# An eight-way output projection replaced by seven products per pair of row tiles, and the state-space stage placed between other gate groups

## The chip, the cores and the metric

The kernel runs on one core of a Trainium2 chip. The metric is the device time of one execution in microseconds (us), from the first to the last instruction of the core. TensorE is PE in the rows, VectorE is DVE, ScalarE is ACT, GpSimd is POOL, and SyncE is SP. SP issues most of the transfers, in one queue in the order in which they are written.

## What is computed

It is one step of a one-layer hybrid decoder for 512 prompt rows and 64 sample rows (576 rows of 1024 values, all in float32). What matters here, with `h = rms_norm(x)`:

```python
z = h @ w_in
u, q, kvc, kvs, kvw, g_nsa, g_a, g_b = jnp.split(z, cuts, axis=-1)
y_ssm, ssm_state = s5_scan(u, h0, ...)          # states, 64 wide, in 32 groups of 16 channels
zg = jax.nn.gelu(y_ssm)
glu = zg * jax.nn.sigmoid(zg @ w_glu + b_glu)
o_nsa = nsa_attention(qh, gh, full_c, full_s, win_ext, ...)
a_br = glu @ w_ssm_out
b_br = o_nsa @ w_nsa_out
merged = jax.nn.sigmoid(g_a) * a_br + jax.nn.sigmoid(g_b) * b_br
x = x + merged @ w_o                              # 576 x 1024 by 1024 x 1024
x = x + hier_moe(rms_norm(x), ...)                # 16 experts, top 2 in one of 4 groups
x = x + jax.nn.sigmoid(x @ w_ple_gate) * (p_l @ w_ple)
y = rms_norm(x) * final_norm_g
```

`s5_scan` has no matrix form of its own. The kernel cuts the 576 rows into 72 chunks of 8 and turns the inside of a chunk into small products, and walks over the chunks with a recurrence on VectorE.

## The kernel before

**One queue per engine.** Every engine runs its own list in the order in which it is written, and the engines meet at semaphores. The TensorE list is the spine. Its results go to a ring of six PSUM banks (`begin` takes the next bank once it has been emptied, `finish` counts up `pe_done`), and `make_plan` says for each result which engine empties it. A row tile is 128 rows (tiles 0 to 3) or 64 rows (tile 4, the samples). Weights pass through three buffers, `w_slot0` to `w_slot2`, in the order of the table `WEIGHTS`. A load waits until the last product with the buffer's former contents is done.

**The input projection and the state-space stage.** After the u and the key and value columns TensorE works through eight gate groups m = 0 to 7 (`gate_products(m)`: ga and gb for 128 features each, two halves of 288 rows, 32 matrix products) and four query groups (`query_products(m, h)`). The short products of the state-space stage stand between them: `x` (transposes of the u rows, which SP has read back from DRAM in chunks as `uc` and VectorE has copied into `ucg`), `vt` (transposes of the input maps `vn`), `k` (the taps, from `bbar` and `gm`), `d` (the drive of each chunk). Then VectorE walks over the 64 prompt chunks, a loop of five short instructions a step, while TensorE does the other gate and query groups, and `y` (the outputs) waits for the walk (`walked`). `KD_A` is the number of gate groups ahead of `x`. `gm`, the output maps, is made by seven GpSimd instructions of 2304 values, at the same time as VectorE makes `bbar` and `vn`. After `y` twelve transposes of no use (`keep_busy(12)`) stand before `zg` (transposes of the activated outputs), then come `fin` and `glu`.

**What follows the last gate group.** The normalized input `hT` is read by the gate groups. Its space is used again for the raw cache pages of the attention stage, so SP holds them back:

```python
            sp.wait_ge(pe_done, PLAN.done(("gb", KD - 1, 1)))
            for s in range(NSEQ):
                load_raw(s)
```

Behind the 16 page loads (`load_raw`, lines 795 and 799, with a table entry read into a register for each) SP issues `pe_r`, `w2`, the weights `w1k0` and `w1k1` (line 723), and at last the final states as two outputs, which count up `fin_out` (lines 814 and 816). ScalarE, VectorE and GpSimd wait for `fin_out` before they write to buffers of the attention stage (in ScalarE's list `act.wait_ge(fin_out, 32)` stands ahead of the first copy into `kvct`). TensorE's transposes `pe` (line 1334) and `ct` 0 to 9 (line 1342) fill at most six banks before ScalarE empties the first, and the compression products (line 1365) need the last `ct` copied.

**The output projection and the router.** `merged` is made on VectorE in 16 pieces from the products `ab` and `bb`. Then `through_w_o(t, c)` makes 128 rows by 512 columns with eight products of 512 columns each, for tiles 0 to 3 and the two halves c of `w_o` (buffers `wo0`, `wo1`), and one group for tile 4 (`("wo", 4, 1)`). `add_w_o` adds each to `x` on VectorE with the factor 0.25. The four halves c = 0 come first. `second_norm_steps` is the table that mixes the rest with the second norm and the router: `xT` (transposes of x), `rt` and `rb` (router logits), `pT` and `pp` (the per-layer embedding), `rank`, `first`, `list` (the sorting of rows by expert). `NORM2` is the order in which the tiles are normalized: ScalarE squares a tile, GpSimd makes the root, ScalarE scales (`hn`), GpSimd writes the rows to DRAM (`h_rows`). When the last tile is written and the first expert's row list is made, GpSimd gathers the first expert's rows, SP waits for them (`hg_ld[0]`) and only then loads the third and later experts' weights.

## Time and profile before

| what | value |
|---|---|
| three timed runs | 814.77, 816.21, 816.44 us (median 816.21) |
| span of the profiled execution | 820.2 us (no other time is recorded for it) |
| TensorE busy | 789.7 us, 96% of the span |
| VectorE, ScalarE, GpSimd busy | 345.2, 193.6, 138.9 us |
| mean granted TensorE clock | 0.992 |
| bytes moved | 136.49 MB, 166 GB/s over the span |

Busy time of TensorE is near the whole span, so the reader looks for the places where TensorE waits and for what stands behind each wait. The profiled execution is 4.0 us longer than the median of the timed ones.

### The profile page before, as it was taken

To read this page: it belongs to the slowest core of one execution; us is meant where nothing else is said; L and a number is where in the kernel's file an instruction comes from. 1 tells how busy PE (TensorE), PEld (TensorE's weight loads), DVE (VectorE), ACT (ScalarE), POOL (GpSimd) and SP (SyncE) were. 2 spreads that over 40 slices of the span, in tenths; PEclk is the share of its full clock that TensorE was granted. 3 is DMA by queue.
4 is the path that set the end of the run, shared out by engine and by line. 5 is a ranking of instruction groups with operands and counts; after the bars stand their busy time and mean duration, and the time that the engine had idled before them with its cause. 6 is when DMAs were issued, how large, how long until landed. Compare 5 with 4: busy or idle time off the path is not lost. (4 is left out here: it accounts for less than half of the span.)

```text
span 820.2 us, 13714 instructions
## 1 busy us (share of the span) xinstructions
PE 789.7 (96%) x5151; PEld 513.4 (63%) x5151; DVE 345.2 (42%) x944; ACT 193.6 (24%) x462; POOL 138.9 (17%) x167
## 2 busy tenths in 40 slices
PE   8999999999999999898999999999999999999995
PEld 6455577877778879655666775445556564554441
DVE  2279911365553332666734363123732101115433
ACT  3010211311111344554523200035211111122222
POOL 3029300500001211234510100012111101014000
PEclk9999999999999999999999999999999999999998
DMA  9540294551411396800030179003699999996011
GB/s 323 146 123 0 81 280 164 145 46 40 172 44 43 109 175 225 225 1 2 1 117 2 59 219 370 2 26 116 226 420 414 418 417 416 416 353 206 26 51 39
DMA packets 81221, 136.49 MB, mean 166 GB/s; under 512 B 33926, under 2 KB 57546, under 8 KB 76946
## 3 DMA queue, kind: packets, MB, share of 16 engines
q1 hardware_dynamic: 64636, 110.17, 40.9%
q0 software_dynamic: 3728, 13.38, 4.6%
q10 hardware_dynamic: 12798, 12.12, 4.4%
q8 instruction: 41, 0.67, 0.3%
q14 instruction: 18, 0.15, 0.1%
HBM read 116.55 MB, written 21.19 MB: 168 GB/s over the span
## 5 line engine op out<-in xcount | busy, mean ns | idle before, releaser
L1170 PE MATMUL ps<-hT,w_slot 128*128 128x288 f32 x640 | 156.2, 407 | 0.0
L1170 PEld LDWEIGHTS ps<-hT,w_slot 128*128 128x128 f32 x640 | 121.3, 190 | 34.1 <-issue 0.8
L1170 PE MATMUL ps<-w_slot,hT 128*128 128x512 f32 (+1 forms) x320 | 127.0, 555 | 0.3 <-DVE hT L1835 0.3
L1170 PEld LDWEIGHTS ps<-w_slot,hT 128*128 128x128 f32 x320 | 60.0, 190 | 61.0 <-issue 42.4
L1170 PE MATMUL ps<-w_slot,merged 128*128 128x512 f32 x128 | 55.9, 593 | 0.0
L1674 PE MATMUL ps<-w_slot,hT 128*32 128x256 f32 x544 | 49.7, 380 | 0.0
L2624 DVE SCALAR_TENSOR_TENSOR th<-th,ps 128x256 f32<-128x256 f32 x12 | 5.1, 422 | 105.2 <-ACT th L2077 105.2
L1170 PEld LDWEIGHTS ps<-w_slot,merged 128*128 128x128 f32 x128 | 24.0, 190 | 28.4 <-issue 28.2
L1043 POOL TENSOR_TENSOR hT<-hT,w_p 128x512 f32<-128x512 f32 (+3 forms) x11 | 25.1, 2282 | 51.2 <-DVE w_p L2150 51.2
L1170 PE MATMUL ps<-qg,w_slot 128*128 128x288 f32 x128 | 33.7, 408 | 0.0
L1674 PEld LDWEIGHTS ps<-w_slot,hT 128*32 128x32 f32 x544 | 26.3, 110 | 10.0 <-issue 2.3
L2410 DVE TENSOR_REDUCE nm_p<-ps 128x2 f32<-128x256 f32 (+3 forms) x32 | 24.9, 819 | 15.9 <-PE ps L1415 15.8
L1170 PE MATMUL ps<-onsaT,w_slot 128*128 128x288 f32 x128 | 31.2, 406 | 0.0
L1662 PE MATMUL ps<-wgu,hT 128*128 128x256 f32 x128 | 28.9, 382 | 0.9 <-DVE hT L2150 0.9
L1674 PE MATMUL ps<-wgu,hT 128*32 128x256 f32 x352 | 28.4, 379 | 0.6 <-DMA w_slot<-in_w_exp_up 0.6
L1985 ACT ACTIVATE hT<-ps,nm_p 128x128 f32<-128x128 f32 (+3 forms) x44 | 22.6, 524 | 25.9 <-DVE nm_p L2410 21.8
L984 POOL TENSOR_SCALAR stat<-stat 128x1 f32<-128x1 f32 (+1 forms) x15 | 3.0, 203 | 151.3 <-ACT qg L2022 93.2
L1170 PEld LDWEIGHTS ps<-onsaT,w_slot 128*128 128x128 f32 x128 | 24.3, 190 | 6.7
L1662 PEld LDWEIGHTS ps<-wgu,hT 128*128 128x128 f32 x128 | 23.9, 190 | 6.7 <-issue 2.5
L2498 DVE SCALAR_TENSOR_TENSOR x<-ps,x 128x512 f32<-128x512 f32 x8 | 5.5, 692 | 50.0 <-PE ps L1170 50.0
L1104 POOL TENSOR_TENSOR tick<-tick 128x1 f32<-128x1 f32 x16 | 3.1, 195 | 138.6 <-PE ps L1645 90.2
L1170 PEld LDWEIGHTS ps<-qg,w_slot 128*128 128x128 f32 x128 | 23.2, 191 | 5.4
(441 smaller groups left out, 1223.1 us busy)
## 6 DMA issues: line engine op xcount, KB each, us to landing
merged<-in_w_exp_down SPq DMA_DIRECT2D x11, 1024.0 KB, 17.1
w_slot<-in_w_in SPq DMA_DIRECT2D x8, 1024.0 KB, 6.9
wgu<-in_w_exp_gate SPq DMA_DIRECT2D x8, 1024.0 KB, 12.8
wgu<-in_w_exp_up SPq DMA_DIRECT2D x8, 1024.0 KB, 15.1
w_slot<-in_w_exp_gate SPq DMA_DIRECT2D x8, 1024.0 KB, 13.1
w_slot<-in_w_exp_up SPq DMA_DIRECT2D x8, 1024.0 KB, 15.6
expert_rows<-onsaT ACTq DMA_DIRECT2D x12, 512.0 KB, 8.0
w_slot<-in_w_exp_down SPq DMA_DIRECT2D x5, 1024.0 KB, 16.1
```

The source lines that it names most:

```text
L984: link(pool.tensor_scalar(stat[0:p, 1, t:t + 1], stat[0:p, 0, t:t + 1], 1.0 / D, EPS, ALU.mult, ALU.add))
L1043: pool.tensor_tensor(p4, p4, w_p[:, i].rearrange("p a b -> p (a b)").unsqueeze(2).broadcast_to([P, 4, n]), ALU.mult).then_inc(pr_scaled, 1)
L1104: pool.tensor_tensor(tick[:, 1:2], tick[:, 0:1], tick[:, 0:1], ALU.add).then_inc(pool_tick, 1)
L1170: ins = pe.matmul(out, a, b, start=(n == 0), stop=(n == len(pairs) - 1))
L1662: ins = pe.matmul(ps[:, 2 + u, FF * w:FF * w + FF], hgT[:, u, k], w0[:, w, k], start=(k == 0), stop=(k == KD - 1))
L1674: ins = pe.matmul(ps[g:g + 32, 2 + u, FF * w:FF * w + FF], hgT[:, u, k, g:g + 32], gate_up_slot(l)[:, w, k], start=(k == 0), stop=(k == KD ...
L1985: ins = act.activation(probs[i % PBUFS][:, (2 * c + kh) * n:(2 * c + kh) * n + n], ps[:, 2 * (at % 2) + kh, 0:n], ACT.Exp, bias=nm_p[:, at ...
L2410: dve.tensor_reduce(nm_p[:, at], ps[:, 2 * (at % 2):2 * (at % 2) + 2, 0:n], axis=X, op=ALU.max, negate=True).then_inc(pr_max, 1)
L2498: empty(dve.scalar_tensor_tensor(v, o[0:TILES[t], :], 0.25, v, ALU.mult, ALU.add))
L2624: dve.scalar_tensor_tensor(th[:, u], th[:, u], 1.0, ps[:, 2 + u, 0:FF], ALU.add, ALU.mult).then_inc(si_made, 1)
```

## The change

There are two parts. **In the state-space stage** `KD_A` goes from 3 to 1: gate group 0 alone stands before `x`, group 1 comes after `d`, groups 2 to 6 after the queries, and group 7 stands behind `y`, where `keep_busy(12)` was. SP issues the read of `uc` ahead of the query weights (it was behind the key and value outputs), loads gate weights `g2` after the taps and `glu` ahead of `g3`. `gm` is made by six VectorE instructions behind `vn` in place of the seven on GpSimd, and the staging of the first gates moves from `xg` to `vt`. **In the output projection** the rows of a pair of tiles (0 and 1, 2 and 3) and the four quarters of `w_o` are combined so that seven products of four matrix products each (128 rows, 512 values of the sum, 512 columns) replace eight of them: 56 matrix products in all in place of 64. Four of a pair's products accumulate in a bank of their own (`ps[:, RING + p]`) with an addition to x between them. VectorE makes the sums (`row_sum`, and four combinations of weights of 2048 values each). Tile 4 goes first, NORM2 becomes (4, 0, 1, 2, 3), and the table mixes the products with the router in a new order. The final gain `gf` and the first two down weights are loaded after `("rt", 2)`.

```diff
-KD_A = 3
+KD_A = 1
...
+    steps = [("wo", 4, 1), ("m", 0, 1), ("m", 0, 2), ("xT", 4, 0), ("xT", 4, 1), ("m", 1, 1), ("rt", 4, 0), ("m", 1, 2), ("rb", 4, 0)]
+    steps += [("m", 0, 5), ("m", 0, 6), ("m", 0, 3), ("m", 0, 7), ("xT", 0, 0), ("xT", 0, 1), ("m", 0, 4), ("rt", 0, 0)]
+    steps += [("m", 1, 5), ("rb", 0, 0), ("xT", 1, 0), ("m", 1, 6), ("xT", 1, 1), ("pT", 0, 0), ("pT", 1, 0), ("m", 1, 3), ("rt", 1, 0)]
+    steps += [("pT", 2, 0), ("pT", 3, 0), ("m", 1, 7), ("rb", 1, 0), ("pT", 4, 0), ("xT", 2, 0), ("xT", 2, 1), ("xT", 3, 1), ("m", 1, 4)]
+    steps += [("rt", 2, 0), ("xT", 3, 0), ("rb", 2, 0), ("pp", 0, 0), ("rt", 3, 0), ("pp", 0, 1), ("rb", 3, 0), ("pp", 1, 0), ("rank", 0, 0)]
+    steps += [("pp", 1, 1), ("first", 0, 0), ("pp", 2, 0), ("list", 0, 0)]
+    return steps + [("pp",) + job for job in PP_JOBS[5:len(PP_JOBS) - PP_LEFT]]
...
+AFTER_W_O = ("rt", 2)
...
             load_weights("g0")
             load_weights("g1")
+            sp.wait_ge(u_out, 16 * NT)
+            sp.wait_ge(v_made, 1)
+            sp.wait_ge(g_made, 1)
+            sp.dma_start(uc, u_dram.rearrange("(c t) n -> c t n", t=CH)).then_inc(uc_ld, 16)
             load_weights("q")
...
-            load_weights("g2")
...
+            load_weights("g2")
+            load_weights("glu")
             load_weights("g3")
-            load_weights("glu")
...
+            gate_products(KD_A)
             for m in range(1, GQA):
                 for h in range(2):
                     query_products(m, h)
-            for m in range(KD_A, KD):
+            for m in range(KD_A + 1, KD - 1):
                 gate_products(m)
             pe.wait_ge(walked, 1)
...
-            keep_busy(12)
+            gate_products(KD - 1)
             pe.wait_ge(y_gelu, 8)
...
+            def w_o_product(p, i):
+                a, b = (slice(P * (2 * p + t), P * (2 * p + t) + P) for t in range(2))
+                low, high = wk("wo0", 512), wk("wo1", 512)
+                rows, weights = {1: (merged[:, 0:4, a], low[:, 0:4]), 2: (merged[:, 4:8, a], low[:, 4:8]), 3: (s_wo[:, 3], high[:, 4:8]),
+                                 4: (merged[:, 4:8, b], low[:, 4:8]), 5: (s_wo[:, 0], t1_wo), 6: (s_wo[:, 1], t2_wo),
+                                 7: (s_wo[:, 2], high[:, 0:4])}[i]
+                if i in (5, 6, 7, 3):
+                    pe.wait_ge(wo_sums, 4 * p + {5: 1, 6: 2, 3: 3, 7: 4}[i])
+                if i in (5, 6, 7, 4):
+                    pe.wait_ge(wo_weights, {5: 1, 6: 2, 7: 3, 4: 4}[i])
+                before = {6: 1, 7: 6, 4: 7, 3: 5}.get(i)
+                if before:
+                    pe.wait_ge(wo_added, ADDED.index((p, before)) + 1)
+                if i == 2:
+                    o = begin(("wo2", p, 2))
+                elif i == 5:
+                    o = begin(("wo2", p, 3))
+                elif i == 3:
+                    o = bank(("wo2", p, 3))
+                else:
+                    o = ps[:, RING + p]
+                for k in range(4):
+                    ins = pe.matmul(o, rows[:, k], weights[:, k], start=(k == 0 and i in (1, 2, 5)), stop=(k == 3), skip_group_check=True)
+                if i in (2, 3):
+                    finish(ins)
+                else:
+                    ins.then_inc(wo_chain, 1)
...
+            n9 = [P, NS, CH + 1, GRP]
+            pr, pi = (pw[:, :, r, :].rearrange("p t s -> p s t").unsqueeze(3).broadcast_to(n9) for r in range(2))
+            c_re, c_im = (cst[:, r].unsqueeze(2).broadcast_to(n9) for r in range(2))
+            tg9 = tmp_g.rearrange("p (s t c) -> p s t c", s=NS, t=CH + 1)
+            tt(gm[:, 0], pr, c_re, ALU.mult)
+            link(tt(tg9, pi, c_im, ALU.mult))
+            tt(gm[:, 0], gm[:, 0], tg9, ALU.subtract)
+            link(tt(gm[:, 1], pi, c_re, ALU.mult))
+            link(tt(tg9, pr, c_im, ALU.mult))
+            dve.scalar_tensor_tensor(gm[:, 1], gm[:, 1], -1.0, tg9, ALU.mult, ALU.subtract).then_inc(g_made, 1)
...
+            def row_sum(p, i):
+                a, b = (slice(P * (2 * p + t), P * (2 * p + t) + P) for t in range(2))
+                low_a, high_a, low_b, high_b = merged[:, 0:4, a], merged[:, 4:8, a], merged[:, 0:4, b], merged[:, 4:8, b]
+                n = 4 * p + {5: 1, 6: 2, 3: 3, 7: 4}[i]
+                first, second, op = {5: (low_b, high_b, ALU.add), 6: (s_wo[:, 0], low_a, ALU.subtract),
+                                     3: (high_a, s_wo[:, 1], ALU.subtract), 7: (low_a, low_b, ALU.subtract)}[i]
+                tt(s_wo[:, {5: 0, 6: 1, 7: 2, 3: 3}[i]], first, second, op).then_inc(wo_sums, 1)
+                dve.wait_ge(wo_sums, n)
+            row_sum(0, 5)
+            for n in range(2):
+                dve.wait_ge(*w_need[f"wo{n}"])
+            tt(t1_wo, high[:, 0:4], low[:, 0:4], ALU.subtract).then_inc(wo_weights, 1)
+            dve.wait_ge(wo_weights, 1)
+            row_sum(0, 6)
+            tt(t2_wo, high[:, 4:8], t1_wo, ALU.subtract).then_inc(wo_weights, 1)
+            dve.wait_ge(wo_weights, 2)
+            row_sum(0, 3)
+            row_sum(0, 7)
...
+            def add_product(p, i):
+                a, b = 2 * p, 2 * p + 1
+                places = {1: [(a, 0)], 2: [(a, 0)], 5: [(b, 1)], 6: [(a, 1)], 3: [(a, 1)], 7: [(b, 1)], 4: [(b, 0)]}[i]
+                if i in (2, 3):
+                    o = take(("wo2", p, i))
+                else:
+                    dve.wait_ge(wo_chain, CHAINED.index((p, i)) + 1)
+                    o = bank(("wo2", p, 3)) if i == 5 else ps[:, RING + p]
+                n = ADDED.index((p, i)) + 1
+                dve.wait_ge(wo_added, n - 1) if n > 1 else None
+                t, c = places[0]
+                v = x[:, t, 512 * c:512 * c + 512]
+                ins = dve.scalar_tensor_tensor(v, o, 0.25, v, ALU.mult, ALU.add).then_inc(wo_added, 1)
+                if i in (2, 3):
+                    dve.wait_ge(wo_added, n)
+                    dve.sem_inc(drained["dve"], 1)
+                return ins
...
+                    add_last_rows()
+                    tt(high[:, 0:4], high[:, 4:8], high[:, 0:4], ALU.subtract).then_inc(wo_weights, 1)
+                elif what == "m":
+                    add_product(t, c)
+                    if (t, c) == (1, 2):
+                        tt(low[:, 4:8], low[:, 4:8], t2_wo, ALU.subtract).then_inc(wo_weights, 1)
+                    elif t == 0 and c in (5, 6, 3, 7):
+                        row_sum(1, c)
```

TensorE, the end of the state-space stage, before: the last `y` products (`vn,xg` and `gm,hst`), the twelve idle transposes, and `zg`, `fin`, `glu`.

```order
L1300 MATMUL ps<-vn,xg 72x128 x8
L1306 MATMUL ps<-gm,hst 72x128 x16
L1188 MATMUL ps<-ident 128x128 x12
L1315 MATMUL ps<-ident,uc 128x72 x32
L1319 MATMUL ps<-ident,fin 128x128 x2
L1321 MATMUL ps<-ident,fin 16x128 x2
```

The same place of the changed kernel, where the row with `hT` is gate group 7:

```order
L1302 MATMUL ps<-vn,xg 72x128 x8
L1308 MATMUL ps<-gm,hst 72x128 x16
L1171 MATMUL ps<-hT,w_slot 128x288 x32
L1317 MATMUL ps<-ident,uc 128x72 x32
L1321 MATMUL ps<-ident,fin 128x128 x2
L1323 MATMUL ps<-ident,fin 16x128 x2
```

The last reader of `hT` has moved from in front of all `y` products to behind them.

SP's queue from the weights of gate group 2 and 3 on (`w_slot1`), before. The 16 rows of line 707 are the query weights.

```order
L695 DMA w_slot1<-in_w_in 128x8x256 x2
L707 DMA w_slot2<-in_w_in 128x4x64 x16
L752 DMA out_2<-kv 128x4x256
L755 DMA out_6<-kv 64x256
L752 DMA out_3<-kv 128x4x256
L755 DMA out_7<-kv 64x256
L752 DMA out_4<-kv 128x4x256
L758 DMA out_8<-kv 8x256 x8
L760 DMA out_8<-in_cache_win_kv 8x4x16384
L767 DMA uc<-u_rows 72x4096
```

And changed:

```order
L713 DMA w_slot1<-in_w_in 128x8x256 x2
L770 DMA uc<-u_rows 72x4096
L725 DMA w_slot2<-in_w_in 128x4x64 x16
L774 DMA out_2<-kv 128x4x256
L777 DMA out_6<-kv 64x256
```

The read of `uc` now stands between two sets of weights, directly ahead of the query weights.

TensorE, the output projection, before: behind the last product from `onsaT` come four halves, then `x` transposes between the others (L1177 is tile 4, L1600 and L1605 the router).

```order
L1170 MATMUL ps<-w_slot,merged 128x512 x32
L1590 MATMUL ps<-ident,x 128x128 x4
L1170 MATMUL ps<-w_slot,merged 128x512 x8
L1590 MATMUL ps<-ident,x 128x128 x4
L1170 MATMUL ps<-w_slot,merged 128x512 x8
L1590 MATMUL ps<-ident,x 128x128 x8
L1177 MATMUL ps<-w_slot,merged 64x512 x16
L1600 MATMUL ps<-hT,w_rt 32x128 x8
```

And changed, where `onsaT` holds the row sums, `qg` and `kv` the weight sums, and L1579 is `w_o_product`:

```order
L1178 MATMUL ps<-w_slot,merged 64x512 x16
L1579 MATMUL ps<-w_slot,merged 128x512 x8
L1622 MATMUL ps<-ident,x 128x64 x8
L1579 MATMUL ps<-w_slot,merged 128x512 x4
L1632 MATMUL ps<-hT,w_rt 32x64 x8
L1579 MATMUL ps<-w_slot,merged 128x512 x4
L1637 MATMUL ps<-groups_sum,actT 64x20
L1579 MATMUL ps<-qg,onsaT 128x512 x4
L1579 MATMUL ps<-kv,onsaT 128x512 x4
L1579 MATMUL ps<-w_slot,onsaT 128x512 x8
```

Tile 4, which needs all of `merged` and both halves of the weights, has become the first group, and the products follow in fours.

## Rows read from the trace of the kernel before

**Rows 1.** The page: span, busy time by engine, transfer rate in 40 slices.

```profile
span 820.2 us, 13714 instructions
...
PE 789.7 (96%) x5151; PEld 513.4 (63%) x5151; DVE 345.2 (42%) x944; ACT 193.6 (24%) x462; POOL 138.9 (17%) x167
...
GB/s 323 146 123 0 81 280 164 145 46 40 172 44 43 109 175 225 225 1 2 1 117 2 59 219 370 2 26 116 226 420 414 418 417 416 416 353 206 26 51 39
```

**Rows 2.** Chain that ended last, in time: start, length, engine or transfer.

```profile
573.56 6.57 DMA h_rows<-hn
...
580.69 4.69 DMA hT<-h_rows,idx
...
587.02 10.88 DMA w_slot<-in_w_exp_up
```

**Rows 3.** TensorE timeline, gate groups 0 to 2, transposes x, drive d.

```profile
96.30 46.83 PE L1170 MATMUL ps<-hT,w_slot 128*128 128x288 f32 x192
142.96 2.17 PE L1251 MATMUL ps<-ident,qg 72*128 72x72 f32 x32
...
158.53 4.22 PE L1285 MATMUL ps<-xg,vt 128*64 128x72 f32 x128
```

**Rows 4.** TensorE timeline from the first y products to the compression.

```profile
263.66 1.91 PE L1300 MATMUL ps<-vn,xg 128*72 128x128 f32 x16
...
278.80 1.53 PE L1188 MATMUL ps<-ident 128*128 128x128 f32 x12
...
284.07 15.76 PE L1170 MATMUL ps<-vt,w_slot 128*128 128x288 f32 x64 [0.50 <-DVE vt L2333]
...
307.42 2.46 PE L1365 MATMUL ps<-kvct,w_slot 128*128 128x161 f32 x16 [1.05 <-ACT kvct L1858]
```

**Rows 5.** SP's issues: query weights, raw pages, compression weights, later pages.

```profile
97.45 14.18 SPq L707 DMA_DIRECT2D w_slot<-in_w_in  x16
...
264.92 18.10 SPq L799 DMA_DIRECT2D hT<-in_cache_cmp_kv  x16
...
285.62 8.06 SPq L723 DMA_DIRECT2D w_slot<-in_cmp_w  x4
...
303.38 18.50 SPq L826 DMA_DIRECT2D caches<-in_cache_slc_kv  x16
```

**Rows 6.** ScalarE timeline, the first copies of the attention stage.

```profile
302.23 5.14 ACT L1858 ACTIVATE kvct<-ps 128x64 f32<-128x64 f32 x11 [1.86 <-DMA out<-fo_p]
```

**Rows 7.** VectorE timeline: small operations, last of vn, copy of uc, end of the walk.

```profile
64.44 9.42 DVE L2150 TENSOR_TENSOR sm<-sm 128x16 f32<-128x16 f32 x3
...
103.56 2.27 DVE L2150 TENSOR_TENSOR vn<-vn,uc 128x2048 f32<-128x2048 f32 x1
...
139.11 2.29 DVE L2275 COPY qg<-uc 72x4096 f32<-72x4096 f32 x1 [33.08 <-DMA uc<-u_rows]
...
257.11 0.31 DVE L2324 TENSOR_TENSOR fin<-fin,cst 128x144 f32<-128x144 f32 x1
```

**Rows 8.** GpSimd timeline, the last of the seven instructions that make gm.

```profile
83.47 6.06 POOL L1006 TENSOR_SCALAR gm<-gm 128x2304 f32<-128x2304 f32 x1
```

**Rows 9.** Line 707, the query weights: time from issue to landing.

```profile
DMA to landing us min/median/max: 3.5/4.3/8.0
```

**Rows 10.** Windows (PE, PEld, DVE, ACT, POOL busy; clock; DMA share; GB/s).

```profile
133.00:135.00 2.00, 2.00 (x10) 1.56 (x9) 0.00 (x0) 0.00 (x0) 0.00 (x0) 1.00 0.52 184
...
336.00:337.00 1.00, 0.93 (x5) 0.78 (x6) 0.01 (x1) 0.99 (x5) 0.00 (x0) 0.50 1.03 201
```

**Rows 11.** TensorE timeline of the output projection: first four, one xT.

```profile
501.25 27.63 PE L1170 MATMUL ps<-w_slot,merged 128*128 128x512 f32 x64
...
568.24 0.64 PE L1590 MATMUL ps<-ident,x 128*128 128x128 f32 x4
```

**Rows 12.** VectorE timeline, last piece of merged, addition of the last product.

```profile
502.01 0.46 DVE L2150 TENSOR_TENSOR merged<-mt 128x288 f32<-128x288 f32 x1
...
568.30 0.69 DVE L2498 SCALAR_TENSOR_TENSOR x<-ps,x 128x512 f32<-128x512 f32 x1 [6.64 <-PE ps L1170]
```

153 lines of the change are left out of this document (71 added, 82 removed).

## The prediction

> **What bounds the kernel now.** I read the page first: TensorE is busy 96% of a span of 820.2 us [rows 1]. So time is won by taking work from TensorE or its waits, and it is lost wherever TensorE is made to wait. Next I read the chain that ended last. Its last part starts at the second norm: the write of the normalized rows, the gather of the first expert's rows, the load of expert weights that SP holds back until the gather has landed [rows 2]. Behind it the expert stage moves 414 to 420 GB/s in six slices on end [rows 1], so transfers pace it as much as TensorE does. A gain ahead of that stage counts only as far as the gather comes earlier. Third I read TensorE's timeline around each edited place, and then the queues of the engines that release it. There the reader is to see one thing above all: a second chain, which TensorE does not show as a wait because its own work is just as long.
>
> That chain starts when the last gate group has been computed, since the raw cache pages go where `hT` was. In the trace TensorE goes on to y at 263.66 [rows 4]. SP starts the page loads 1.26 us later, at 264.92, and spends 18.10 us on 16 of them, 1.13 us each. That price does not depend on the place, as the later 16 pages cost 18.50. At 285.62 come the compression weights, 8.06 us [rows 5], then the final states as outputs, for whose landing ScalarE waits until 302.23 with the first copy into kvct [rows 6]. The copies take 5.14 us, and the compression starts at 307.42, after only 1.05 us of visible idle time [rows 4]. So from the end of the gates to the compression there are 307.42 − 263.66 = 43.76 us of a chain of SP and ScalarE. TensorE has filled it with y (15.14 us, up to 278.80), the idle transposes, zg, fin, 15.76 us of glu [rows 4], and the transposes.
>
> **The change part by part.**
>
> *Group 7 behind y.* All y products move in front of the gates' end. With an otherwise unchanged list that end falls at 278.80 in place of 263.66: +15.14 us. The 43.76 us behind it are all issues, landings and copies that this edit leaves as they are, so the compression starts 15.14 us later too. TensorE then has only zg, fin and glu as cover, to about 19.5 us after the gates' end (the 15.76 of glu and what stands from 278.80 + 1.53 to 284.07), the transpose pe and five banks of ct. Then it waits for ScalarE's first copy, which comes 302.23 − 263.66 = 38.57 us after the gates' end. What is late next is everything: VectorE and GpSimd wait for the same landing, and the caches' loads stand behind it in SP's queue. The idle transposes (1.53 us) that go away are worth nothing, as the glu stage no longer ends on the path. Neither does the earlier walk gain: it needs to 257.42 [rows 7], y stood at 263.66, and now it has some 25 us of slack that nobody uses.
>
> *One gate group ahead of x.* TensorE reaches x at 96.30 + 46.83/3 = 111.91, not at 142.96 [rows 3]. For that u must be back in chunks. Today uc lands at 139.1 [rows 7]. Two things move it forward. VectorE's small operations ran at about 3 us each, as in 9.42 us for three, while GpSimd made gm, to 89.53 [rows 7, 8]; without these neighbours the part up to vn is shorter by some 30 us. I take it so that vn is done near 76 instead of 105.8. The six new VectorE instructions have 2304 values; at 2.27 us for 2048 [rows 7] they take 2.55 us each, 15.3 in all, so gm is there at about 91, ahead of SP's 97.45 [rows 5]. That edit I cost at nothing. But uc (1.18 MB) now goes in front of the query weights. Those are issued from 97.45 for 14.18 us [rows 5] and the last lands at 111.6 + 3.5 or later [rows 9], 115.1; TensorE wants them after x, at 111.9 + 2.0 = 113.9. The bare lateness is 1.2 us. To it comes the time of uc: at the 420 GB/s of the best slice [rows 1] 2.8 us; at the 184 GB/s while uc itself was moving [rows 10] 6.4 us, and the landing may be the median 4.3 instead of 3.5. That gives a wait between 1.2 (uc beside the others) and 8.4 us. I take 5.5, between the two prices of uc. The copy of uc, 2.29 us [rows 7], ends close to TensorE's arrival and stays under this wait.
>
> The Trainium skill (DMA: Bandwidth & Descriptors, section Why a DMA increments its semaphore by 16 and not by 1) says that a transfer is spread over the largest number of engines up to 16 that divides its outer dimension. For the 72 rows of uc these would be 12, and an estimate by that page with three quarters of the best rate is 3.7 us for uc, a wait of 4.9 us. The 0.52 share of the engines in that window neither shows nor excludes it [rows 10].
>
> *The clock.* After short idle times the granted clock is 0.50 in the slice from 336 [rows 10], that is 1.2 in place of 2.4 GHz, and three such slices follow each other. Two long waits are new. I price the first at 1.5 us (three slices at half rate), the second at 1.0, since ScalarE paces the transposes there. Bounds: 0 and 4 together.
>
> *Seven products in place of eight.* Four whole products take 27.63 us with the overlap of one, thus 3.4 us for four matrix products [rows 11]. 56 instead of 64 matrix products save 6.9 us of TensorE. At the start, tile 4 needs the last piece of merged, which ends at 502.47 [rows 12] while TensorE is free at 501.25 [rows 11]: 1.3 us lost. Row sums of 512 values (0.7 us, like an addition of 0.69 of that size) and weight sums of 2048 (2.3 us [rows 7]) are on VectorE, which sat idle 6.64 us ahead of such an addition [rows 12]; the first such product comes some 22 us after the merge, 9 us of sums are ready by then. The chained bank needs each addition (0.7 us) before the next product into it, and other work of 3.4 us stands between, except at product 4 of the first pair, where two xT of up to 0.64 us each [rows 11] cover about all. So no further wait there.
>
> But what counts is the last tile. Before, the last product ended at 568.2, as its addition starts at 568.30 [rows 12], and the rows' write was issued at 573.56, 5.4 us later [rows 2]. In the new table five pT (two transposes each), one more xT (four, 0.64 us with its overlap [rows 11]), one rt and two rb stand ahead of the last product. I take them at 0.27 us each on average, 2.4 us: it ends at 568.2 − 6.9 + 1.3 + 2.4 = 565.0. Behind it ScalarE's list has the copies of tile 2 and 3 ahead of the squares of tile 3. The copy of tile 3 waits for its transpose, and this for rt of tile 2, which waits for ScalarE too. That costs 1.3 us more than before. The write then starts at 565.0 + 5.4 + 1.3 = 571.7 against 573.56: about 1.9 us earlier, and I take 2.0. The first expert's list is ready a little sooner than the write, as before. The gather, the weights behind it and the expert stage come 2.0 us earlier. The other 3.6 us of TensorE's saving become idle time ahead of the experts. Bounds: 0 (the saving is all eaten by the added steps) and 6.9 − 1.3 = 5.6 us.
>
> **The sum** against the profiled span: 15.1 + 5.5 + 2.5 − 2.0 = +21.1 us, 841.3. The span is 4.0 us above the median of the runs, 816.21; I take the difference as it is: 837.3 us. Ends: 15.1 + 1.2 + 0 − 5.6 = +10.7, 826.9; 15.1 + 8.4 + 4.0 − 0 = +27.5, 843.7.
>
> **Rivals.** A: all of TensorE's saving in the projection arrives, since the write's 6.57 us and the gather also shorten or the lists don't block. For it: TensorE alone is then 5.6 us earlier. Against it: ScalarE's order. 833.7 us, chance 0.12. B: the projection gives nothing, because VectorE's additional 14 us of sums delay the additions. Against it: the 6.64 us of idle time ahead of an addition [rows 12]. 839.3 us, 0.10. C: gm on VectorE comes late, because the operations are slow for another reason than GpSimd: vn at 105.8, gm at 121, uc and the query weights 23 us later than assumed. TensorE then waits until some 139, and the whole is 17 us more than forecast, 855 us. The end of the slow operations together with GpSimd's last speaks against it [rows 7, 8]. 0.06. D, the other side: SP's chain gets shorter once nothing but zg and glu runs beside it, page loads at half their cost and the 8.06 us of weight issues nearly gone. It decides from the point where page loads to fin_out take under about 22 us in place of 37; then TensorE bounds the start of the compression, group 7 only changes places with y, and the idle transposes (1.5 us) are saved. With query weights nearly in time (1.2) and 2.0 to 5.6 us of the projection that is 816.2 − 1.5 + 1.2 − 3.8 = 812.1. The unchanged 1.13 to 1.16 us a page at two places with different neighbours [rows 5] speaks against it. 0.04. That the edit does not delay the pages at all is excluded by the list: the semaphore counts results in order, and group 7 is behind y.
>
> **How the numbers follow.** The forecast has 0.68. Its own range by the bounds is 827 to 844, which holds A and B as well, so 828 to 844 leaves out C, D and the tails, under 2 in 10. A measurement of this kernel can tell about 0.2% (1.6 us) from no change. Faster by more: D, 0.04. Within: 0.01. Slower: 0.95.
>
> **What would show it.** In the changed trace: the last gate product ends near 285; SP's first page load 1.3 us behind it; TensorE idle for some 13 us at the ct transposes, released by ScalarE's kvct copy, and about 3 us at pe; the compression 43 to 45 us behind the gates' end, near 330. Before that, a wait of about 5 us at the first query product for the weights, gm on VectorE done at 91, no VectorE operation of 16 values over 0.3 us. In the projection: 3.4 us for four matrix products, 1.3 us of wait at tile 4, the write of the last tile 2 us closer to the end of bb than now (72.3 us), and idle time ahead of the first expert. The prediction is wrong if the compression follows the gates' end in much less than 43 us, or if the distance from bb's end to the first expert shrinks by more than 4 us.

## The result, and the profile of the changed kernel

The changed kernel takes 845.37 us in the median of 4 runs (843.72 to 849.00), against 816.33 us for the kernel before (4 runs beside it): ratio 1.0344, 95% interval 1.0315 to 1.0373. That is 29.0 us slower. The prediction said 837.3 us, 21.1 us slower, with a range of 828 to 844: the sign was right, the size was 8 us too small, and the time lies 1.4 us outside the range. The run that was profiled took 849.0 us, the slowest of the four, with a span of 847.3 us, 27.1 us more than the span before. First the page: span, busy time by engine, the transfer rate in 40 slices.

```profile
span 847.3 us, 13694 instructions
...
PE 790.6 (93%) x5123; PEld 512.9 (61%) x5123; DVE 347.5 (41%) x968; ACT 194.0 (23%) x462; POOL 107.2 (13%) x160
...
GB/s 332 122 119 0 143 224 106 175 80 29 141 43 15 66 128 210 229 106 1 1 33 80 2 186 356 61 14 64 236 403 410 419 416 416 417 363 183 27 50 37
```

TensorE is busy as long as before (790.6 against 789.7 us) in a span that is 27.1 us longer [rows 1]. It has less work now, so part of this busy time is a lower clock; the loss is waits and what the clock costs behind them, and the timeline of TensorE says where they are. This is the beginning, after the first gate group (start, length; in brackets the idle time ahead and what ended it).

```profile
112.55 2.23 PE L1252 MATMUL ps<-ident,qg 72*128 72x72 f32 x32 [1.83 <-DVE qg L2327]
120.46 6.43 PE L1171 MATMUL ps<-hT,w_slot 128*128 128x288 f32 x16 [5.68 <-DMA w_slot<-in_w_in]
126.73 3.66 PE L1264 MATMUL ps<-ident,vn 128*128 128x128 f32 x32
```

Two waits, 1.83 us for the copy of `uc` and 5.68 us for the query weights, and behind the second the 16 query products take 6.43 us where they take 4.15 at full clock. The window over them shows why: granted clock 0.59, so most of them ran at the lower level of 1.2 GHz after the idle time (columns as in [rows 10]; the second window is from the later, longer wait).

```profile
121.00:126.00 5.00, 5.00 (x13) 3.51 (x12) 0.00 (x0) 0.00 (x0) 0.00 (x0) 0.59 0.69 236
311.00:322.00 11.00, 2.28 (x13) 2.04 (x11) 0.00 (x0) 0.00 (x0) 0.00 (x0) 0.66 1.39 164
```

What is behind the first wait is in VectorE's row, and behind the second in SP's: `uc` is issued at 96.15 and its copy starts at 110.20, 14.05 us later; the 16 transfers of the query weights take 20.01 us to issue, where they took 14.18 [rows 5].

```profile
95.03 0.99 SPq L713 DMA_DIRECT2D w_slot<-in_w_in  x2
96.15 1.33 SPq L770 DMA_DIRECT2D uc<-u_rows  x1
97.53 20.01 SPq L725 DMA_DIRECT2D w_slot<-in_w_in  x16
...
110.20 2.29 DVE L2327 COPY qg<-uc 72x4096 f32<-72x4096 f32 x1 [11.85 <-DMA uc<-u_rows]
```

The first row is a neighbour that matters: two loads of gate weights, 2 MB together, issued just ahead of `uc` in the same queue. The trace also has the packets of the transfers. `uc` travels in 72 packets of 16,384 bytes, and the two windows below count none of them from 96 to 102 us and all of them from 102 to 109.5 (the packets of 8 KB or more are 1109 − 1037 = 72).

```profile
DMA packets 1934, 1.96 MB, mean 327 GB/s; under 512 B 16, under 2 KB 1934, under 8 KB 1934
DMA packets 1109, 1.59 MB, mean 212 GB/s; under 512 B 843, under 2 KB 1037, under 8 KB 1037
```

So of the 14.05 us some 6.0 are the wait behind the gate weights, 7.3 the packets of `uc` (102.2 to 109.5), and 0.7 the rest. The packets of the query weights (256 bytes each) last from 102.4 to 120.0 us, 17.5 us, where they took 10.7 before (103.6 to 114.2). The 6.8 us more are nearly the 7.3 us of `uc` between them.

Further up, VectorE's three operations of 16 values that took 9.42 us [rows 7] take 0.47:

```profile
54.77 0.47 DVE L2192 TENSOR_TENSOR sm<-sm 128x16 f32<-128x16 f32 x3
```

Before, five operations of 16 values took 4.1 to 5.5 us each while GpSimd made `gm`. In the kernels where VectorE makes it, none takes over 0.26 us.

Next the same stretch of TensorE as in [rows 4], from the first y products to the compression, with the issue of the raw pages by SP and ScalarE's first copy.

```profile
257.01 1.91 PE L1302 MATMUL ps<-vn,xg 128*72 128x128 f32 x16
...
272.15 15.79 PE L1171 MATMUL ps<-hT,w_slot 128*128 128x288 f32 x64
287.77 2.46 PE L1317 MATMUL ps<-ident,uc 72*128 72x72 f32 x32
...
309.04 0.24 PE L1336 MATMUL ps<-ident,hT 64*128 64x64 f32 x1 [1.88 <-DMA hT<-in_cmp_pe]
...
324.81 4.53 PE L1344 MATMUL ps<-ident,hT 128*128 128x128 f32 x20 [11.53 <-ACT kvct L1890]
...
330.75 2.46 PE L1367 MATMUL ps<-kvct,w_slot 128*128 128x161 f32 x16
...
289.04 17.19 SPq L816 DMA_DIRECT2D hT<-in_cache_cmp_kv  x16
...
324.53 4.64 ACT L1890 ACTIVATE kvct<-ps 128x64 f32<-128x64 f32 x10 [16.84 <-DMA out<-fo_p]
```

y takes its 15.14 us (257.01 to 272.15), then comes group 7, the gates end at 287.77, SP's pages start 1.27 us behind, and the compression follows 42.98 us behind the gates' end, where it was 43.76 [rows 4]. The last rows are from the projection and the router: TensorE's wait for tile 4, its last product, the write of the last tile's rows and the gather of the first expert's.

```profile
525.93 7.09 PE L1178 MATMUL ps<-w_slot,merged 128*64 128x512 f32 x32 [1.20 <-DVE merged L2192]
...
586.51 3.60 PE L1579 MATMUL ps<-w_slot,merged 128*128 128x512 f32 x8
...
596.58 0.53 POOL L1079 DMA_DIRECT2D h_rows<-hn  x1 [1.87 <-ACT hn L2066]
605.04 1.40 POOL L1093 DMA_INDIRECT hT<-h_rows,idx  x1 [7.92 <-DMA h_rows<-hn]
```

bb ends 1.20 us ahead of 525.93, at 524.73, so the write is issued 71.85 us behind bb's end (before 72.31 [rows 2, 11]) and the gather 80.31 us behind it (79.44). The forecast wanted 2.0 us less in both.

### The profile page after: what moved, and what is told of

The parts are those of the page before. It is cut to its first block and busy times, and to the rows that moved or that the text cites. A ratio compares the mean times of both kernels' runs of the same rounds, so it can differ in the third digit from the quotient of the medians.

```text
span 847.3 us, 13694 instructions
## 1 busy us (share of the span) xinstructions
PE 790.6 (93%) x5123; PEld 512.9 (61%) x5123; DVE 347.5 (41%) x968; ACT 194.0 (23%) x462; POOL 107.2 (13%) x160
## 5 line engine op out<-in xcount | busy, mean ns | idle before, releaser
L1171 PE MATMUL ps<-hT,w_slot 128*128 128x288 f32 x640 | 158.8, 411 | 5.7 <-DMA w_slot<-in_w_in 5.7
L1940 ACT ACTIVATE qg<-ps 128x288 f32<-128x288 f32 x28 | 11.5, 412 | 95.9 <-PE ps L1171 95.9
L1738 PE MATMUL ps<-merged,actT 128*32 128x512 f32 x144 | 25.4, 595 | 1.0 <-DMA merged<-in_w_exp_down 0.5
L1020 POOL MEMSET w_slot<- 64x2048 f32 x4 | 7.1, 1804 | 145.2 <-PE ps L1171 145.2
L1890 ACT ACTIVATE hT<-ps 128x512 f32<-128x512 f32 (+1 forms) x15 | 7.9, 556 | 76.3 <-PE ps L1622 73.8
L1706 PEld LDWEIGHTS ps<-wgu,hT 128*32 128x32 f32 x352 | 15.5, 110 | 14.3 <-issue 4.1
## 6 DMA issues: line engine op xcount, KB each, us to landing
wgu<-in_w_exp_up SPq DMA_DIRECT2D x8, 1024.0 KB, 15.1
```

Of the source, the lines that this page charges most:

```text
L1171: ins = pe.matmul(out, a, b, start=(n == 0), stop=(n == len(pairs) - 1))
L1706: ins = pe.matmul(ps[g:g + 32, 2 + u, FF * w:FF * w + FF], hgT[:, u, k, g:g + 32], gate_up_slot(l)[:, w, k], start=(k == 0), stop=(k == KD ...
L1738: ins = pe.matmul(ps[g:g + 32, 4 + c, :], actT[:, u, f, g:g + 32], down_slot(l)[:, f, 512 * c:512 * c + 512], start=(f == 0), stop=(f == 1))
L1890: empty(act.activation(dst, src, ACT.Copy))
L1940: empty(act.activation(stage[:, n % 4, w], o[:, 0:HALF], ACT.Tanh, scale=0.5))
```

## The experiments

Times on a chip are compared with runs of the kernel before on the same chip; its median there was 817.9 to 818.7 us, so the ratios count, and 0.001 is 0.82 us. The profiled executions differ among themselves too, by up to 4.5 us in the attention stage and up to 6 us from the gather to the end, so the distances inside a stage carry the argument more than spans do. In fifteen of the sixteen later profiles the first gate group starts at 94.6 to 94.9 us, where [rows 3] has 96.30. The trace of before was 1.4 us late at its start; without this lateness (the common scale below) its compression stood at 306.0.

**1. The state-space part alone.** The changed kernel with the projection as before, the start of its diff against the change:

```diff
-NORM2 = (4, 0, 1, 2, 3)
+NORM2 = (0, 1, 4, 2, 3)
...
+            for t in range(NT - 1):
+                through_w_o(t, 0)
```

> The kernel before with the state-space part of the change alone (one gate group ahead of x, group 7 behind y, gm on VectorE, uc ahead of the query weights); the projection is as before. In the trace of the whole change the compression started 23.3 us later than before, and the span grew by 27.1 us, so 3.8 us come behind it. Theory 1, the 3.8 us belong to the projection part: here the compression starts 23.3 us later and nothing is added behind it, 839.6 us (838 to 841). Theory 2, the 3.8 us come with the late start itself (transfers in the expert stage and at the end meet others): 842 to 845 us.

Measured: 844.05 us, ratio 1.0312 (1.0289 to 1.0336). The compression starts at 329.40, 23.4 us behind 306.0, as both theories say. Both theories count from 816.33 us, and there the ratio gives 841.8 us (839.9 to 843.8). That is between the two and separates neither. But some 25.5 of the 28 us are there without the projection part, so that part isn't what makes the change slow.

**2. The projection part alone**, with the state-space stage as before, the start of its diff against before:

```diff
-NORM2 = (0, 1, 4, 2, 3)
+NORM2 = (4, 0, 1, 2, 3)
...
+                elif what == "m":
+                    w_o_product(t, c)
```

> The kernel before with the projection part alone (seven products for a pair of row tiles, the new table, ScalarE's order); the state-space stage is as before. Forecast by the prediction: 2.0 us faster, 814.3 us. Theory 1 (the 3.8 us belong to this part): 820 us. Theory 2: the first expert's weights come about 1 us late and the list 0.2 us early, as in the trace of the whole change, and nothing more: 816 to 817 us, no difference to be seen.

Measured: 818.49 us, ratio 1.0003 (0.9984 to 1.0022). The forecast's 2.0 us (ratio 0.9976) are outside the interval, and so are the 3.8 us of theory 1. It gives nothing; theory 2 stands.

**3. Group 7 ahead of y again**, all else as in the change.

```diff
-            for m in range(KD_A + 1, KD - 1):
+            for m in range(KD_A + 1, KD):
                 gate_products(m)
...
-            gate_products(KD - 1)
+            keep_busy(12)
```

> The whole change, but gate group 7 stands ahead of y again (and the 12 idle transposes behind y are back); group 0 alone stays ahead of x. Theory (the page loads wait for the last gate group, and y's 15.14 us stood between): the gates' end moves from 287.8 to about 272.7, the compression still follows 43 us behind, 845.4 - 15.1 = 830.3 us. Rival (SP's chain has another beginning, for example the glu weights or the end of the short stage): 840 us or more.

Measured: 827.12 us, ratio 1.0105 (1.0080 to 1.0129).

```profile
271.81 1.91 PE L1301 MATMUL ps<-vn,xg 128*72 128x128 f32 x16
...
286.94 1.53 PE L1188 MATMUL ps<-ident 128*128 128x128 f32 x12
...
314.82 2.46 PE L1366 MATMUL ps<-kvct,w_slot 128*128 128x161 f32 x16 [0.99 <-ACT kvct L1889]
```

```profile
273.07 17.19 SPq L815 DMA_DIRECT2D hT<-in_cache_cmp_kv  x16
```

The gates end at 271.81, the pages start 1.26 us behind, the compression 41.75 us behind the pages. In all seventeen profiles that last distance is 41.0 to 42.5 us (42.50 in [rows 4, 5]), with the pages anywhere from 263 to 294: the chain of SP and ScalarE moves as one piece with the last gate group, whatever TensorE does beside it. The compression is 15.9 us earlier than in the change, and the time fell by about 19 us, where the theory had 15.1 (830.3 us, ratio 1.017). So the page loads do hang on the last gate group, and the rival is excluded, but about 4 us of the gain are not explained by it.

**4. The query weights ahead of `uc`.**

```diff
+            load_weights("q")
             sp.wait_ge(u_out, 16 * NT)
             sp.wait_ge(v_made, 1)
             sp.wait_ge(g_made, 1)
             sp.dma_start(uc, u_dram.rearrange("(c t) n -> c t n", t=CH)).then_inc(uc_ld, 16)
-            load_weights("q")
```

> The whole change, but the query weights are issued ahead of the load of uc. In the trace of the change the issue of their 16 transfers took 20.0 instead of 14.2 us with uc ahead, and uc took 12.7 us to land. Theory 1 (they share the queues; whoever is first delays the other by about as much): the query weights land near 115, uc near 118, x starts near 120 and the first query product right behind, no wait for weights but as much for uc: 844 to 847 us. Rival (uc alone makes the wait of 5.7 us and would be quick behind the weights): x near 115, 840 to 842 us.

Measured: 848.67 us, ratio 1.0371 (1.0351 to 1.0391). The 844 to 847 us of theory 1 are a ratio of 1.034 to 1.038, so this is theory 1: no wait for weights, but 11.84 us ahead of x.

```profile
122.49 4.10 PE L1252 MATMUL ps<-ident,qg 72*128 72x72 f32 x32 [11.84 <-DVE qg L2327]
```

**5. The whole change once more.** 

> The whole change once more, to see what of the last 4.5 us belongs to it. In its first profile the first transpose of x for the last stage came 4.38 us behind that stage's first product, and the second 13.39 us behind the first; before 1.96 and 11.74; with the stage part alone 4.62 and 13.42, with the query weights first 3.58 and 11.74. Theory 1 (these waits for the gathers of the experts' rows differ from execution to execution, the change has no part in them): one or both distances come out otherwise here, and the ratio stays between 1.031 and 1.037. Theory 2 (the change moves these transfers): 4.4 and 13.4 again.

Measured: 846.00 us, ratio 1.0341 (1.0309 to 1.0373). The two distances are 3.99 and 11.74 us now: theory 1 for the second, undecided for the first. Over all seventeen profiles the first is 1.9 to 4.6 and the second 11.7 or 13.3 to 13.4, in versions with and without either part (before 1.96 and 11.74, the state-space part alone 4.62 and 13.42). These rows of the first profile show what happens there. TensorE waits for VectorE's x, and VectorE for the gathers of the experts' rows; this wait makes the first distance. Behind it the granted clock falls once (0.66 over 766 to 771 us), and this makes the second: it is 13.3 to 13.4 us in the five profiles in which the clock falls there (the change, 1, 6, 12, 13) and 11.7 in the twelve others.

```profile
765.62 1.25 PE L1806 MATMUL ps<-ident,x 128*128 128x128 f32 x8 [2.50 <-DVE x L2192]
```

```profile
766.00:771.00 5.00, 5.00 (x15) 1.79 (x15) 1.45 (x2) 1.79 (x3) 3.17 (x5) 0.66 0.78 248
```

**6. Another order in the projection.** The kernel before with the projection part; `pT` and the embedding products `pp` stand behind the last product, and ScalarE makes the squares of tile 3 first.

```diff
-    steps += [("pT", 2, 0), ("pT", 3, 0), ("m", 1, 7), ("rb", 1, 0), ("pT", 4, 0), ("xT", 2, 0), ("xT", 2, 1), ("xT", 3, 1), ("m", 1, 4)]
+    steps += [("m", 1, 7), ("rb", 1, 0), ("xT", 2, 0), ("xT", 2, 1), ("xT", 3, 1), ("m", 1, 4)]
+    steps += [("rt", 2, 0), ("xT", 3, 0), ("rb", 2, 0), ("pT", 0, 0), ("pT", 1, 0), ("rt", 3, 0), ("pT", 2, 0), ("rb", 3, 0), ("pT", 3, 0), ("pT", 4, 0)]
+    steps += [("pp", 0, 0), ("pp", 0, 1), ("pp", 1, 0), ("rank", 0, 0)]
...
-            turned_half(3)
             squares(3)
+            turned_half(3)
```

> The kernel before with the projection part, but the five turns pT and all embedding products stand behind the last product of the projection, behind rt and rb of tile 3, and ScalarE makes the squares of tile 3 ahead of its copy of that tile's transposes. Projection part alone: bb's end to the last product 64.17 us (after the wait), from there to the landing of the rows 14.04. Theory (the added steps ahead of the last product and ScalarE's order eat TensorE's saving; the landing of the last rows releases the experts' weights): 62.2 and 12.5 us, the weights and the list about 3 us earlier than with the projection part alone, 815.5 us on the scale of 818.5, ratio 0.9965. Rival (the list or the embedding products then wait): ratio 1.000.

Measured: 820.80 us, ratio 1.0031 (1.0011 to 1.0052), slower than both theory and rival. The write came earlier, and the gather did not.

```profile
566.64 0.53 POOL L1095 DMA_DIRECT2D h_rows<-hn  x1 [1.86 <-ACT hn L2080]
577.25 1.07 POOL L1109 DMA_INDIRECT hT<-h_rows,idx  x1 [10.07 <-DVE idx L2205]
```

The write is issued 68.88 us behind bb's end (497.76), 3 us earlier than in experiment 2, but GpSimd now waits for VectorE's indices, not for the landing. I had put three embedding products, 5.39 us, ahead of the ranks. The rival was right about the mechanism: two things start the expert stage, the landed rows and the list. Its ratio of 1.000 is outside the interval, though. The gather stands where it stood in experiment 2 (79.49 and 79.40 us behind bb's end), so why this order is some 2 us slower than experiment 2 is not shown.

**7. `uc` from ScalarE's queue.**

```diff
-            sp.dma_start(uc, u_dram.rearrange("(c t) n -> c t n", t=CH)).then_inc(uc_ld, 16)
...
+            act.dma_start(uc, u_dram.rearrange("(c t) n -> c t n", t=CH)).then_inc(uc_ld, 16)
             for m in range(KD_A):
                 take_gates(m, stage_a)
```

> The whole change, but uc is loaded by ScalarE's queue, ahead of its first gate copies, and no longer by SP between the gate and the query weights. Theory (uc in front of the query weights stretches SP's issue of their 16 transfers from 14.2 to 20.0 us, and uc itself takes 14 us to be there): gm is done at 88.4, uc lands near 101, the issue takes 14.2 us again, the waits at x (1.8 us) and at the first query product (5.7) shrink to 1 us together, and the query product has the full clock again (2.3 us). The gates' end moves from 287.8 to about 279, ratio 1.024. Rival (moving the query weights themselves takes that long): ratio 1.034.

Measured: 842.62 us, ratio 1.0319 (1.0283 to 1.0355). ScalarE was busy with copies of `kv` until 95.9 and issued it only at 97.31, so nothing was earlier, and the query weights took 21.62 us to issue. So it doesn't test an earlier `uc`, but it shows that the stretching doesn't depend on `uc` being in SP's queue.

**8. Three repairs:** experiments 3, 6 and 7 in one kernel. 

> The change with three repairs: group 7 ahead of y, uc from ScalarE's queue, and the projection's other order. Group 7 ahead of y gave ratio 1.0105. With about 8.5 us less at the start and 3 us less at the projection: 815.8 us where before has 818.7, ratio 0.996. Rival (the start of the page loads is not earlier than before, since TensorE had no wait up to there): the best case is the kernel before with the projection part, so not under 0.996 either; if the early part costs anything, ratio 1.000 to 1.003.

Measured: 829.46 us, ratio 1.0137 (1.0114 to 1.0161), neither theory: two of the three repairs were none, as 6 and 7 show. It comes out 2 to 3 us slower than experiment 3, which has the third repair alone (the intervals overlap); why is not shown.

**9. `uc` from GpSimd's queue**, which waits for nothing else at that time.

```diff
-            sp.dma_start(uc, u_dram.rearrange("(c t) n -> c t n", t=CH)).then_inc(uc_ld, 16)
...
+            pool.wait_ge(g_made, 1)
+            pool.dma_start(uc, u_dram.rearrange("(c t) n -> c t n", t=CH)).then_inc(uc_ld, 16)
```

> The whole change, but uc is loaded from GpSimd's queue, which is free as soon as gm is made (88.4 us), 9 us ahead of ScalarE's and 8 us ahead of SP's issue in the earlier runs. There uc landed 12 to 14 us after its issue and the 16 transfers of the query weights took 20.0 to 21.6 us to issue. Theory (uc and the query weights share the transfer engines from 96 to 110; it does not matter whose queue holds uc): uc lands near 99, x starts without a wait at 110.7, the issue of the query weights takes about 15 us and the first query product waits 0 to 1 us. The gates' end moves from 287.8 to about 279.5, ratio 1.024. Rival (uc takes until the query weights are there wherever it is issued, or the query weights are slow by themselves once gm's stage has ended): ratio 1.032 again.

Measured: 836.26 us, ratio 1.0216 (1.0176 to 1.0256). GpSimd's issue, VectorE's copy, SP's query weights, TensorE:

```profile
88.70 0.67 POOL L1008 DMA_DIRECT2D uc<-u_rows  x1 [71.03 <-DVE gm L2321]
```

```profile
98.00 2.28 DVE L2327 COPY qg<-uc 72x4096 f32<-72x4096 f32 x1
```

```profile
97.02 13.03 SPq L725 DMA_DIRECT2D w_slot<-in_w_in  x16
```

```profile
110.28 2.17 PE L1252 MATMUL ps<-ident,qg 72*128 72x72 f32 x32
113.24 4.15 PE L1171 MATMUL ps<-hT,w_slot 128*128 128x288 f32 x16 [0.79 <-DMA w_slot<-in_w_in]
```

With nothing queued ahead of it `uc` landed 8.5 us after its issue, 6.5 us of them packets. The query weights take 13.03 us to issue, x starts without a wait, and the query products wait 0.79 and take 4.15 us. The gates end at 278.27 instead of 287.77: 9.5 us were the price of `uc` between the gate weights and the query weights. The compression starts at 321.14, 15.1 us behind 306.0. That is y's own time, 15.14 us; nearly nothing else is left.

**10. The list early.** Experiment 6 with one embedding product ahead of the ranks, one ahead of the first rows, two ahead of the list.

```diff
-    steps += [("pp", 0, 0), ("pp", 0, 1), ("pp", 1, 0), ("rank", 0, 0)]
-    steps += [("pp", 1, 1), ("first", 0, 0), ("pp", 2, 0), ("list", 0, 0)]
+    steps += [("pp", 0, 0), ("rank", 0, 0), ("pp", 0, 1), ("first", 0, 0)]
+    steps += [("pp", 1, 0), ("pp", 1, 1), ("list", 0, 0), ("pp", 2, 0)]
```

> The order of the sixth experiment (kernel before with the projection part), but only one embedding product stands ahead of the ranks, one ahead of the first rows and two ahead of the list. There the rows' write was issued at 566.64, but the first gather waited until 577.25 for VectorE's indices, which stood behind 4.2 us of embedding products. Theory (the expert stage starts when both the last rows have landed and the list is made): gather near 573.9, 3.3 us earlier than there and 2 us earlier than with the change's own order; ratio 0.998. Rival (the gather is only one of the things that the start waits for): ratio 1.002 or more.

Measured: 817.41 us, ratio 0.9986 (0.9965 to 1.0007). bb ends at 501.00 and the gather follows 77.25 us behind it, 2.2 us less than before and 2.2 less than in experiment 2; experiment 6 had 79.49. The time excludes the rival's 1.002, and can't tell the theory's 0.998 from no change.

```profile
569.87 0.53 POOL L1095 DMA_DIRECT2D h_rows<-hn  x1 [1.85 <-ACT hn L2080]
578.25 1.42 POOL L1109 DMA_INDIRECT hT<-h_rows,idx  x1 [7.85 <-DMA h_rows<-hn]
```

**11. All repairs:** experiments 3, 9 and 10 in one. 

> The change with group 7 ahead of y, uc from GpSimd's queue and the projection in the order of the tenth experiment. Theory: TensorE has no wait up to the gates' end, which comes within 1 us of the kernel before, so this is as fast as the tenth experiment, ratio 0.998. Rival (something of the early group is still paid): ratio 1.003 to 1.008.

Measured: 817.79 us, ratio 0.9994 (0.9976 to 1.0012); compression at 305.88, where before (on the common scale) has 306.0. The rival's 1.003 to 1.008 is excluded: the early group costs nothing that can be measured when `uc` comes early, and it gains nothing either.

**12. y ahead of group 7, alone,** in the kernel before.

```diff
-            for m in range(KD_A, KD):
+            for m in range(KD_A, KD - 1):
                 gate_products(m)
...
-            keep_busy(12)
+            gate_products(KD - 1)
```

> The kernel before with one edit: y stands ahead of gate group 7 (and the idle transposes are gone); three groups stay ahead of x. The walk was done at 257.4 in the profile of before, while y would come at 248: TensorE waits 8 to 9 us for it, then y (15.1 us) and group 7. Theory (everything in SP's chain hangs on the last gate group): the gates' end moves by 15.1 + 8.5 us, the compression by as much, ratio 1.029. Rival (the wait lets ScalarE's and VectorE's work or SP's transfers catch up, so part comes back): ratio 1.02.

Measured: 845.06 us, ratio 1.0315 (1.0281 to 1.0349), the theory. TensorE waits for the walk and then runs at the lower clock (the first 16 products of y take 3.69 us, where they took 1.91). All of it arrives at the compression: 331.54, 25.5 us behind 306.0.

```profile
255.98 3.69 PE L1301 MATMUL ps<-vn,xg 128*72 128x128 f32 x16 [9.14 <-DVE fin L2326]
```

**13, 14, 15. The load of gf.** The change also moved the load of the final norm's weights (512 KB) from bb's end to just ahead of the experts' down weights, about 5 us ahead of the last rows' write. These three kernels move it behind the first held-back expert weights: in experiment 10, in experiment 11, and in the whole change.

```diff
-            sp.dma_start(gf, I["final_norm_g"].rearrange("(o n) -> o n", o=1).broadcast_to([P, D])).then_inc(gf_ld, 16)
             for u in range(2):
                 load_down(u, u)
...
             load_down(2, expert(2))
+            sp.dma_start(gf, I["final_norm_g"].rearrange("(o n) -> o n", o=1).broadcast_to([P, D])).then_inc(gf_ld, 16)
```

> The tenth experiment (kernel before with the projection part, list early), but the load of gf stands behind the first held-back expert weights instead of ahead of the experts' down weights. Theory (gf's 512 KB stand in the queues ahead of the last rows' write): from the write's issue to the gather 7.1 us as before instead of 8.4, ratio 0.997. Rival (the landing is slow for another reason, for example the write before it, 2.5 us earlier): 8.4 us again, ratio 0.9986.

> The eleventh experiment (all repairs) with gf's load moved in the same way. There the write took 8.5 us to the gather. Theory: 7.1 us, 1.3 us earlier, ratio 0.998. Rival: no change, 0.9994.

> The whole change with only gf's load moved behind the first held-back expert weights. Theory: from the write's issue (596.58 in the change) to the gather 7.1 instead of 8.5 to 8.9 us, the held-back weights 1.3 us earlier, ratio 1.0325. Rival: 8.5 us or more, ratio 1.034.

Measured: 817.57 us and 0.9988 (0.9966 to 1.0010); 816.89 us and 0.9982 (0.9964 to 0.9999); 843.48 us and 1.0309 (1.0280 to 1.0339). From the write's issue to the gather: 7.17 us in 14 and 7.29 in 15.

```profile
568.72 0.53 POOL L1079 DMA_DIRECT2D h_rows<-hn  x1 [1.83 <-ACT hn L2065]
575.89 1.06 POOL L1093 DMA_INDIRECT hT<-h_rows,idx  x1 [6.64 <-DMA h_rows<-hn]
```

```profile
596.35 0.53 POOL L1079 DMA_DIRECT2D h_rows<-hn  x1 [1.87 <-ACT hn L2066]
603.64 1.06 POOL L1093 DMA_INDIRECT hT<-h_rows,idx  x1 [6.76 <-DMA h_rows<-hn]
```

GpSimd's wait for this landing was 6.59 to 6.76 us in all five profiles that have gf elsewhere and wait for it (before, 1, 12, 14, 15), and 6.77 to 8.36 us in the nine that have it there (7.92 and 8.36 in the change). The two ranges nearly touch; their means are 6.6 and 7.5 us. So the theory holds for the landing, at 0.8 us on average. The times can't settle it: in 13 and 14 the interval holds both values, in 15 it ends at the rival's. In 13 it gave no time, since the gather then waited for the list instead (8.21 us for the indices). Experiment 14 is the fastest version, and its interval ends just under 1: 1.4 us better than the kernel before, if anything.

## Why the prediction was wrong in size

Here is the profile of the change against the one of before at the same places, beside the forecast.

| place | forecast | measured | what it is |
|---|---|---|---|
| start of the stage | 0 | −1.4 | before's own profile was late |
| y ahead of group 7 | +15.1 | +15.1 | y's own time |
| `uc` ahead of the query weights, waits | +5.5 | +7.5 | 1.83 at x, 5.68 at the queries |
| clock behind the wait, and rest of the stretch | +1.5 | +2.8 | 6.43 against 4.09 us, small remainders |
| gates' end to compression | +1.0 | −0.8 | chain 0.8 us shorter |
| compression | +23.1 | +23.3 | |
| bb's end to the gather | −2.0 | +0.9 | projection, write, gf |
| compression to bb's end, and gather to the end | 0 | +2.9 | clock, gathers of the last rows |
| sum of the spans | +21.1 | +27.1 | |

The compression came out within 0.2 us of the forecast, and that is luck. The waits and the clock at the start were 3.3 us too small, and the late start of before's profile (1.4) and the shorter chain (1.8) happened to make up for it. On the common scale the compression is 24.7 us late, 1.6 more than forecast. The medians are 29.0 us apart, 8 more than forecast: 1.6 up to the compression, 2.9 from the projection, and about 3.4 that no row places (below). So the steps that failed are the time around `uc` and the gain of the projection, and the rest is a zero that I put down for everything behind.

**The chain behind the gates' end** was right in its place, its mechanism and its size. It was the main term. Experiments 3, 9 and 12 show it. ScalarE's copy releases the transposes, as forecast (11.53 us there, 1.88 at pe); page loads 1.27 us behind the gates' end (forecast 1.3). The granted clock did fall in this wait (0.66 over the 11 us from 311), but ScalarE paces what follows, so the 1.0 us I put down for it was not paid: the chain got shorter instead.

**The step "that wait is between 1.2 and 8.4 us, I take 5.5"** hit the wait (5.68) and missed its neighbours. I priced `uc` by its bytes, 2.8 to 6.4 us, and let its copy stay "under this wait". Its packets took 7.3 us, not far from the upper price. What I left out is what stood ahead of it in the queue: 2 MB of gate weights, 6.0 us. From issue to copy it takes 14.05 us here, at most 9.3 with nothing queued ahead (experiment 9), 9.7 behind the query weights (4), 12.3 beside them (7). In the kernel before it took 17.8, and its own issue row would have said so:

```profile
120.35 0.83 SPq L760 DMA_DIRECT2D out<-in_cache_win_kv  x1
121.30 0.38 SPq L767 DMA_DIRECT2D uc<-u_rows  x1
```

There a copy of 2 MB stands directly ahead of it, and its 72 packets are spread from 123.4 to 138.5 us. I read its landing [rows 7] and not the distance to its issue. So x waited as well, and the query products ran at 1.2 GHz. Experiment 9 takes nearly all of it away: 9.5 us at the gates' end, against the 7.0 forecast. The Trainium skill (DMA: Bandwidth & Descriptors, section Why a DMA increments its semaphore by 16 and not by 1) led me to an estimate of 3.7 us for `uc`. No run here comes near it: the packets of `uc` alone took 6.5 us at the least (experiment 9) and 7.3 us in the change, and the measurement decides.

**The step "the write then starts 1.9 us earlier, and I take 2.0"** failed. Three things were mis-sized. TensorE's last product ended 65.4 us behind bb's end, against 67.0 before: 1.6 us won where I had 3.2. With 6.9 us saved and 1.2 waited at tile 4, the turns, transposes and router steps put ahead of it, with a wait of 0.50 us for VectorE, took 4.1 us, not 2.4. ScalarE's order cost 1.2 us, as forecast, so the write came 0.46 us earlier, not 2. And gf's load, moved in front of the experts' down weights, delayed the landing by 0.2 to 1.8 us. I had given this moved load no cost at all. Rival B (the projection gives nothing) had the right outcome by the wrong cause: the sums on VectorE fit into its idle time, and TensorE waited only 0.50 us for VectorE among these products. Experiments 10 and 14 show that the seven products do bring something, 2.2 and 3.4 us at the gather, once both releases of the expert stage are early.

**Behind that**, the forecast's "the expert stage comes as much later" left out what differs between executions. In the profile of the change the last stage came 4.1 us later by the two distances of experiment 5 than in the one of before, 2.4 us of waiting and 1.7 us of lower clock; before's waits there were nearly the smallest of all. But the medians, which don't hang on one execution, say 28 to 29 us. With y ahead of group 7 (the change twice, experiments 1, 4, 7, 9, 12, 15) the time, by the ratios, exceeds the shift of the compression by −0.6 to 3.4 us, 1.9 on average; without it (3, 8, 11, 14) by −1.5 to 0.8, −0.3 on average. That suggests about 2 us more that hang on the late gates' end somewhere behind the compression. It is not shown. Each of these numbers is uncertain by some 2 us. In the profiles the stretch from the compression to the end lasts 509.8 to 516.5 us with y ahead (eight) and 508.4 to 516.1 without (nine), with means only 1.1 us apart. No row shows a cause; it stays open.

Rival A is excluded by the gather; C by gm, done at 88.35 (forecast 91), and by operations of 16 values of at most 0.26 us: their slowness went away with GpSimd's seven instructions, as forecast. D is excluded by the fixed 41.0 to 42.5 us.

## What to carry to other kernels

When a buffer is free for loads only after the last of a group of products, the last of that group is the start of a second chain. Count from there, and put nothing ahead of it that could fill the time behind. A transfer's time from issue to consumer has two parts. One is what stands ahead of it in the queue (6.0 us here), the other its own movement (7.3 us), and the transfers behind it pay for the second (here 6.8 us). Its bytes give at best the second part. And in a diff that moves work, list every moved issue, down to a half-megabyte load that nobody waits for; then look for all the conditions that start the next stage, since making one early only hands the wait to the other.
